# Late weight tiles in slices of 24 matmuls at every second step of two attention stages

## What is computed

```python
a_q, a_k, a_v, a_f, b_q, b_k, b_v, c_in, gate_in = _split_cols(h @ w_in, IN_SPLITS)
# A: FoX, 8 heads of 64: softmax(q k^T / 8 + d_q - d_k, causal) v
out_a = _fox_attention(fq, k_all, v_all, d_all[:, p_len:], d_all, qpos, kpos)
# B: differential attention, 4 heads of 2 x 64, with partial rotary
pd = p[:, :, 0] - lam * p[:, :, 1]
out_b = _rmsnorm(o_b, diff_subln) * (1.0 - lam_init)
# C: RWKV-7 on c_in, then branch gates, output projection, cross-attention, SwiGLU
```

## Time and profile before

| | us |
|---|---|
| median of 3 runs | 3387.74 (3385.36 to 3401.25) |
| profiled execution, device time | 3391.04 |
| its span | 3389.5 |
| FoX stage, layer 1 and layer 2 | about 190 and 189 |
| differential stage, layer 1 and layer 2, from its first product | about 187 and 187 |
| TensorE busy | 2958.4, 87% of the span |
| VectorE busy | 1596.0, 47% |
| ScalarE busy | 720.2, 21% |
| mean granted TensorE clock | 0.939 of full |

### The profile page before, as it was taken

One profiled execution on the slowest core, in us unless ns is written; L12 is line 12 of the kernel. 1 busy time (PEld: TensorE's weight loads), 2 busy tenths in 40 slices (PEclk: granted clock), 3 DMA queues, 4 the chain that ended last, 5 costly groups with the idle time before them and its releaser, 6 DMA issues.

```text
span 3389.5 us, 69793 instructions
## 1 busy us (share of the span) xinstructions
PE 2958.4 (87%) x26572; PEld 2728.0 (80%) x26572; DVE 1596.0 (47%) x2964; ACT 720.2 (21%) x1777; POOL 243.6 (7%) x418
## 2 busy tenths in 40 slices
PE   4879798899979989999966997988988898899997
PEld 3867677788968868999966776778887897699997
DVE  3434344366665226554253444535666742455533
ACT  1023233222211141000011332322222122200001
POOL 1011111100000010000000111110010000000000
PEclk8989899899989999999987998989999999899999
DMA  3333233522134212232223323333221431132221
GB/s 105 109 106 84 87 113 61 161 71 62 49 108 123 78 56 75 87 87 77 73 71 99 102 72 106 111 80 117 82 67 46 139 105 58 51 93 87 84 81 55
DMA packets 420588, 294.58 MB, mean 87 GB/s; under 512 B 38369, under 2 KB 386049, under 8 KB 419777
## 3 DMA queue, kind: packets, MB, share of 16 engines
q1 hardware_dynamic: 397056, 225.19, 23.9%
q0 software_dynamic: 23232, 65.36, 5.9%
HBM read 234.28 MB, written 56.23 MB: 86 GB/s over the span
## 4 chain that ended last, share of the span: by engine, by line
PE 74%; DVE 10%; issue 4%; DVEq 4%; DMA 3%; ACT 3%; POOLq 1%; ACTq 1%; SPq 0%; POOL 0%
PE PS L637 30%; PE PS L705 9%; PE PS L993 6%; PE PS L934 5%; PE PS L615 4%; PE PS L591 2%; PE PS L1138 2%; ACT U L1249 2%; DVE WLO L1739 2%; PE PS L653 2%; PE PS L859 2%; PE PS L749 1%; PE PS L784 1%; PE PS L972 1%; DMA U<-in_rwkv_g_dram 1%
## 5 line engine op out<-in xcount | busy, mean ns | idle before, releaser
L637 PE MATMUL PS<-U_r,WHI 128*128 128x272 f32 x2656 | 487.9, 295 | 63.4 <-DVEq L1740 28.5
L1729 DVE CAST WHI<-ring 128x1024 fp32r<-128x1024 f32 (+2 forms) x292 | 189.6, 649 | 673.5 <-PE PS L637 497.7
L1252 ACT COPY U<-PS 128x272 f32<-128x272 f32 (+9 forms) x774 | 269.3, 372 | 942.8 <-PE PS L993 142.4
L637 PEld LDWEIGHTS PS<-U_r,WHI 128*128 128x128 f32 x2656 | 396.6, 193 | 72.9 <-issue 42.1
L637 PE MATMUL PS<-brT_r,WHI 128*128 128x272 f32 x1728 | 360.6, 290 | 1.9 <-ACTq L1638 1.9
L637 PE MATMUL PS<-U_r,WLO 128*128 128x272 f32 x1696 | 356.5, 292 | 0.0
L637 PE MATMUL PS<-hT_r,WHI 128*128 128x272 f32 x1696 | 349.6, 288 | 0.0
L1739 DVE TENSOR_TENSOR WLO<-ring,WHI 128x1024 fp32r<-128x1024 f32 (+2 forms) x292 | 332.2, 1138 | 22.8 <-issue 0.9
L934 PE MATMUL PS<-U_r,WHI 128*128 128x272 f32 x768 | 240.2, 313 | 49.9 <-POOLq L381 25.6
L637 PE MATMUL PS<-brT_r,WLO 128*128 128x272 f32 x1344 | 278.2, 288 | 0.0
L637 PEld LDWEIGHTS PS<-brT_r,WHI 128*128 128x128 f32 x1728 | 275.2, 191 | 2.3 <-ACTq L1638 2.3
(11 more groups left out here) (318 smaller groups left out, 4466.0 us busy)
## 6 DMA issues: line engine op xcount, KB each, us to landing
ring<-in_w_in_dram SPq DMA_DIRECT2D x126, 512.0 KB, 4.0
ring<-in_w_ffn_in_dram SPq DMA_DIRECT2D x88, 512.0 KB, 3.8
ring<-in_w_ffn_out_dram SPq DMA_DIRECT2D x32, 448.0 KB, 3.3
proj_scratch<-U POOLq DMA_DIRECT2D x104, 136.0 KB, 2.0
U<-proj_scratch SPq DMA_DIRECT2D x48, 272.0 KB, 4.1
gate_scratch<-U POOLq DMA_DIRECT2D x96, 136.0 KB, 2.6
U<-gate_scratch SPq DMA_DIRECT2D x48, 272.0 KB, 2.8
ring<-in_w_branch_dram SPq DMA_DIRECT2D x48, 256.0 KB, 3.0
```

The source lines that it names most:

```text
L637: ins = mm(PS[:, 2 * q + h, 0:HT], w, half(x, h), start=(first and k == 0 and n == 0), stop=(last and k == kn - 1 and n == len(terms) - 1))
L1252: return act.copy(out, in_)
L1729: copy(hi, src)
```

## The change

In the FoX stage the late call stands in the even steps only, with 24 matmuls. In a differential head the calls stand after the first rotary product (as before), once instead of twice after the transposes, not at all after the key transposes, in steps 0, 2, 4 and 6 instead of 0 to 7, not ahead of the sums of squares, and after them (as before); each has 24 matmuls. Only TensorE's program is edited. ScalarE, VectorE, SP and POOL keep their orders and their wait values.

```diff
@@ -692,19 +692,17 @@
 
                 def late(s):
 
-                    n, h, k0 = s // 4, s % 4 // 2, s % 2 * 4
+                    n, h = s // 2, s % 2
                     v = V_LATE + n
-                    if k0 == 0:
-                        if h == 0:
-                            pe.wait_ge(split_done, l * SPLITS + v + 2)
-                        pe.wait_ge(late_evac, l * 2 * N_LATE + 2 * n + h + 1)
-                    for k in range(k0, k0 + 4):
+                    if h == 0:
+                        pe.wait_ge(split_done, l * SPLITS + v + 2)
+                    pe.wait_ge(late_evac, l * 2 * N_LATE + 2 * n + h + 1)
+                    for k in range(8):
                         xhi, xlo = of_h_split(k)
                         whi, wlo = (w[:, v % 2, k, :] for w in (WHI, WLO))
                         for i, (w, x) in enumerate(((whi, xhi), (whi, xlo), (wlo, xhi))):
                             ins = mm(PS[:, 7, 0:HT], w, half(x, h), start=(k == 0 and i == 0), stop=(k == 7 and i == 2))
-                    if k0 == 4:
-                        ins.then_inc(late_done, 1)
+                    ins.then_inc(late_done, 1)
 
                 for it in range(FOX_HEADS // 2):
                     g = pe.snap(l * 4 + it)
@@ -799,8 +797,8 @@
                             fox_prologue(1)
                         if k < 10:
                             fox_scores(k)
-                        if k < 12:
-                            late(12 * it + k)
+                        if k < 12 and k % 2 == 0:
+                            late(6 * it + k // 2)
                         if 2 <= k <= 11:
                             jobs_of.append(job[0])
                             fox_turn(k - 2)
@@ -813,7 +811,7 @@
                     g = pe.snap(l * 2 + it)
                     for h in range(2):
                         pe.wait_ge(df_loaded[h], (g + 1) * 16 * 5)
-                        s0 = 4 * 12 + 14 * (2 * it + h)
+                        s0 = 2 * 12 + 7 * (2 * it + h)
 
                         for i, src in enumerate((DQ, DK)):
                             if i == 0:
@@ -833,7 +831,6 @@
                             ins = tr(PS[:, 5, t * P:(t + 1) * P], DPK[:, h, t, :], ident)
                         ins.then_inc(df_turned, 1)
                         late(s0 + 1)
-                        late(s0 + 2)
                         pe.wait_ge(df_rotated, g * 4 + 2 * h + 2)
                         pe.wait_ge(df_put, g * 18 + 9 * h + 1)
                         for t in range(4):
@@ -842,7 +839,6 @@
                         pe.wait_ge(df_put, g * 18 + 9 * h + 2)
                         tr(PS[0:32, 5, 0:P], DVR[:, h, SEQ:T], ident)
                         tr(PS[0:32, 5, P:2 * P], DK[:, h, SEQ:T], ident).then_inc(df_turned, 1)
-                        late(s0 + 3)
                         pe.wait_ge(df_put, g * 18 + 9 * h + 4)
                         settle(pe)
 
@@ -905,18 +901,18 @@
                                 values(0)
                             if k < 5:
                                 scores(k)
-                            late(s0 + 4 + k)
+                            if k % 2 == 0:
+                                late(s0 + 2 + k // 2)
                             if 2 <= k <= 6:
                                 turn(k - 2)
                             if k >= 4:
                                 values(k - 3)
 
-                        late(s0 + 12)
                         pe.wait_ge(df_sq, g * 2 + h + 1)
                         for s in range(2):
                             ins = mm(PS[:, s, 0:HT], ones[:, :], half(DTMP, s), start=True, stop=True)
                         ins.then_inc(df_sum, 1)
-                        late(s0 + 13)
+                        late(s0 + 6)
                 phase_end(pe, l, 3)
 
 
```

## The result

The changed kernel takes 3469.55 us (median of 4 runs, 3465.11 to 3473.4) against 3387.71, a ratio of 1.0233 with a 95% interval of 1.0202 to 1.0264. It is slower by 82 us, where 56 were forecast; the time lies in the forecast range of 3398 to 3475, near its upper end. The profiled execution took 3472.76, its span 3471.2.

A forecast was written before the change was run, and what follows sets the result against it. TensorE, busy 87% of the span, was taken as the bound. FoX waits 27, differential waits 2 and clock 27 made 56 us on 3391, 3447; with the median 3.3 below the profiled execution, forecast 3444, range 3398 to 3475.

The forecast's parts named there:

- FoX waits: FoX stage: TensorE waits that lose their cover, 3.8 us per turn, 3.4 after joins, 27 us for 8 turns.
- the late call of step 2: FoX step 2: the 24 matmuls wait for ScalarE's copy behind exp(1), 0.5 us per turn.
- the prologue: FoX step 4: second head's prologue waits for copy put(1) behind exp(3) and late_put, 1.3 us, 1.0 of it new.
- scores(8): FoX step 8: scores wait for VectorE's fox_evac(0) behind a split; wait grows from 2.0 to about 3.0 us.
- the late call of step 10: FoX step 10: the late call waits for ScalarE's copy behind exp(9), 1.3 us per turn.
- the overlay: The new order laid over the second FoX turn's durations to find waits losing cover; steps 6, 9 and 11 stay covered.
- Differential waits: Differential heads: 2.8 us of new waits, waits of 1.0 and 1.2 gone; 0.2 us longer per head, 2 for 8.
- Clock: Both stages: more falls to 1.2 GHz, 12 us in FoX and 15 in the heads, 27 together; bounds 0 to 55.
- The joins: Both stages: joining two late calls of 12 into one saves 0.06 us per call that goes, at most 0.20.
- Waits without clock: Rival: the waits come but bring no further low clock; 29 us more, 3417; chance 0.27.
- Cancelling: Rival: 29 us of new waits, but half of the low-clock time, 28 us, goes; 3389, no change; chance 0.16.
- the faster case: Rival: dense calls keep the clock up, waits stay under 10 us, 28 us of clock loss returns; 3364; chance 0.07.

The follow-up runs named there:

- early_split: The changed kernel with VectorE's split of a FoX turn's second tile moved ahead of the reduce of step 7: 3427.11 us, ratio 1.0094.
- after_fill: The changed kernel with 14 useless matmuls in the 2.9 us wait before scores(8) of each FoX turn: 3452.14 us, ratio 1.0187.
- before_fill: The kernel before the change with 12 useless matmuls in its 2.0 us wait before scores(8) of each FoX turn: 3391.5 us, ratio 1.0011.

## Why the prediction was right, and where it was off

**FoX waits: right, place by place.** Forecast 0.5 at the late call of step 2, 1.3 in the prologue, 3.0 at scores(8), 1.3 at the late call of step 10. Measured in the first turn 0.57, 1.29, 2.92 and 1.28; the prologue's is 1.6 at its longest. The waits were forecast at 30 us (27 with the joins taken off), the rows show 31. Steps 6, 9 and 11 stayed covered, as the overlay had it.

**Differential waits: right.** Forecast were 0.9 at the first scores (0.9), 1.1 at the sums of squares (0.8), 0.6 more at the second call (1.0 now against 0.5), and the waits at L859 and L823 gone, as they are. The term was 2 us, the rows show 2.

**Clock: right in kind, too small.** This is the step that was mis-sized: "one more fall in each FoX turn at 1.46", 12 us, and scores(4) at the low level, 15. The rows give 37 and 22, or 52 in all if the waits' 33 are taken from the 85. In FoX I priced a fall by one call of 12. After the change a fall at step 8 takes 1.1 to 2.5 us from the call (4.29 to 5.74, against 3.21 with the fillers) and another 0.3 to 0.9 from the scores before it, and in all eight turns step 4 has one too (calls of 4.03 to 5.25). In the differential heads scores(4) fell to the low level as forecast, but scores(3) mostly did too (1.57 and 1.58 in the fourth head, 0.84 and 1.45 before), and the call behind them took 4.0 to 5.1 us for 3.0. The upper bound, 55 for the clock, was about what came, and the granted clock that was to show it, 0.88 to 0.90, came out at 0.85 and 0.86. That the time still lies in the range is owed to the width of the clock's bounds, not to its estimate.

**The joins** were taken at 0.06 us each. Behind scores a call of 24 takes 3.06 to 3.08 at full rate, two calls of 12 take 3.12 (1.56 each), so 0.04 to 0.06 for a join there. The rule of the Trainium skill, "TensorE: Matmul & The Clock Gate", on what happens when a matmul is issued, by which in a stream only the columns count, gives 0; these rows speak mildly against it. In the total the two can't be told apart.

**The rivals.** Waits without clock would have been 3417: the clock of 0.85 and 0.86 speaks against it, and so do early_split, with more time gone than wait, and after_fill, with 29 us gone from FoX though nothing was done earlier. Cancelling and the faster case needed the clock to rise with longer calls; it fell from 0.92 and 0.93 to 0.85 and 0.86 in FoX. The advice of the Trainium skill, in "TensorE: Matmul & The Clock Gate", in its table of why this matters for kernels, to keep TensorE busy continuously is borne out here in FoX of the changed kernel: the calls of 24 were paid with bare steps, and the filled wait took the clock from 0.85 and 0.86 to 0.92. In the kernel before, filling the wait changed no total.

## What to carry to other kernels

Filler work between the steps of a pipeline should be placed by what the next wait needs, not spread or lumped evenly: the same matmuls in the same total took 453 us or 375 to 380 us for two FoX stages, by where ScalarE's copy and VectorE's split stood. When work on one engine is moved earlier, move its consumers in the other engines' orders too; a finished result that waits behind an instruction for something later is a wait made by order alone. And a wait of TensorE can cost more than its length: here 16 us of wait at one place took 42 us with it. It need not: behind the wait of 2.0 us in the kernel before two turns of eight kept the full rate, and behind one of 0.9 all did.

## What the runs showed of the hardware

The price of standing still was larger than I had expected: 8 waits of 2.9 us, 23 us in all, filled but for 0.8 each with useless matmuls, made the two stages 29 us shorter though nothing was done earlier (granted clock 0.85 and 0.86 to 0.92). The fall behind a wait isn't fixed by the wait's length: the same 2.0 us in the kernel before was followed by calls of 12 that took from 1.70 to 3.02. And the same instructions can take a different time with nothing changed in them: the differential stage of the kernel before took 199.6 to 207.5 us in the runs that kept it, at granted clocks from 0.91 to 0.87. A gain seen in one stage of one profiled execution, 9 us in before_fill, is therefore not yet a gain of the kernel; in 12 runs it had none.
